# The last group of the down projection: two token tiles one behind the other, and the final weighing on VectorE alone

## The reference

```python
xs = xs + g2x[:, None, :] * _swiglu(_modulate(_rmsnorm(xs, norm2_g[l]), sh2x, sc2x), w_ff1[l], w_ff3[l], w_ff2[l])
...
return _rmsnorm(xs, final_g)          # final norm of every token

def _rmsnorm(x, g):
    xf = x.astype(jnp.float32)
    y = xf * lax.rsqrt(jnp.mean(xf * xf, axis=-1, keepdims=True) + EPS)
    return (y * g.astype(jnp.float32)).astype(x.dtype)
```

## Time and profile before

| | us |
|---|---|
| median of 3 runs | 1735.04 |
| the three runs | 1739.56, 1731.56, 1735.04 |
| the profiled execution | 1731.98 |
| its span | 1730.0 |

### The profile page before, as it was taken

The page is one execution under the profiler, slowest core; times in us unless marked ns, Lnnn a source line. Parts: engine busy times, 40 slices in busy tenths (PEclk is TensorE's granted clock), DMA queues, the critical chain, the costliest instruction groups (busy, mean ns, idle before and its releaser), DMA issues.

```text
span 1730.0 us, 23409 instructions
## 1 busy us (share of the span) xinstructions
PE 1696.5 (98%) x8360; PEld 1428.7 (83%) x8360; DVE 1278.2 (74%) x1809; ACT 689.3 (40%) x1132; POOL 454.4 (26%) x407
## 2 busy tenths in 40 slices
PE   6999999999999999999999999999999999999997
PEld 3798988989898888888888888888888888888885
DVE  6587636565457667776789846888887889789998
ACT  7534241422333213445555414443334333434444
POOL 1002020200212000111121200065463655565551
PEclk9999999999999999999999999999999999999999
DMA  9111110212059133787776634156556555887652
GB/s 343 49 50 37 62 49 25 80 41 74 13 188 310 63 97 111 261 278 251 252 268 207 220 111 146 38 176 229 213 201 248 181 207 206 297 285 247 205 170 98
DMA packets 145424, 284.93 MB, mean 165 GB/s; under 512 B 9362, under 2 KB 96034, under 8 KB 141506
## 3 DMA queue, kind: packets, MB, share of 16 engines
q1 hardware_dynamic: 115314, 177.30, 30.6%
q0 software_dynamic: 30032, 106.59, 17.4%
HBM read 205.68 MB, written 78.17 MB: 164 GB/s over the span
## 4 chain that ended last, share of the span: by engine, by line
PE 87%; DVE 6%; DMA 3%; issue 2%; ACT 1%; SPq 0%; POOL 0%; DVEq 0%; ACTq 0%
PE PD L2493 14%; PE PD L2941 11%; PE PM L2941 11%; PE PM L2816 6%; PE PD L2816 6%; PE PD L2978 5%; PE PM L2978 5%; PE PD L2847 4%; PE PD L2624 4%; PE PD L2509 4%; PE PM L2697 2%; DMA g_ring<-g_dram 2%; PE PD L2637 1%; PE PM L2877 1%; PE PD L2877 1%
## 5 line engine op out<-in xcount | busy, mean ns | idle before, releaser
L1091 POOL TENSOR_TENSOR wm_lo<-wm_lo,wm_hi 128x1024 fp32r<-128x1024 f32 x35 | 92.9, 2666 | 79.5 <-ACT wm_hi L1598 78.9
L2493 PE MATMUL PD<-R_hi,whi 128*128 128x512 f32 x352 | 110.2, 394 | 0.0
L2493 PE MATMUL PD<-R_lo,whi 128*128 128x512 f32 x352 | 108.6, 390 | 0.0
L2493 PE MATMUL PD<-R_hi,wlo 128*128 128x512 f32 x352 | 108.5, 389 | 0.0
L2262 DVE TENSOR_TENSOR ws_lo<-S,ws_hi 128x512 fp32r<-128x512 f32 x76 | 82.7, 1099 | 24.3 <-ACT ws_hi L1533 24.3
L942 POOL TENSOR_TENSOR kw<-ktok,hc 128x1280 f32<-128x1280 f32 x8 | 18.4, 2323 | 286.8 <-DVE ktok L1946 286.8
L1533 ACT ACTIVATE ws_hi<-S 128x512 fp32r<-128x512 f32 x76 | 47.7, 627 | 90.7 <-DVE S L2276 66.3
L2402 DVE TENSOR_TENSOR fm_lo<-fm_lo,fm_hi 128x512 fp32r<-128x512 f32 x70 | 79.1, 1130 | 0.7 <-ACT fm_hi L1605 0.7
L2493 PEld LDWEIGHTS PD<-R_hi,wlo 128*128 128x128 f32 x352 | 66.1, 188 | 14.0
L2493 PEld LDWEIGHTS PD<-R_lo,whi 128*128 128x128 f32 x352 | 66.1, 188 | 13.9
L2493 PEld LDWEIGHTS PD<-R_hi,whi 128*128 128x128 f32 x352 | 65.2, 188 | 12.9 <-issue 0.2
(11 more groups left out here) (532 smaller groups left out, 5353.2 us busy)
## 6 DMA issues: line engine op xcount, KB each, us to landing
rawF<-in_w_ff SPq DMA_DIRECT2D x44, 512.0 KB, 6.2
wm_lo<-w_dram SPq DMA_DIRECT2D x35, 512.0 KB, 3.9
ada<-in_w_ada POOLq DMA_DIRECT2D x32, 512.0 KB, 5.5
raw<-in_w_in SPq DMA_DIRECT2D x30, 512.0 KB, 5.2
g_dram<-snapG POOLq DMA_DIRECT2D x48, 256.0 KB, 4.8
f_dram<-Fo SPq DMA_DIRECT2D x11, 1024.0 KB, 5.6
w_dram<-job_a POOLq DMA_DIRECT2D x20, 512.0 KB, 3.7
fm_lo<-fs_dram SPq DMA_DIRECT2D x40, 256.0 KB, 4.1
```

The costliest lines, as they stand in the source:

```text
L1091: nc.gpsimd.tensor_tensor(lo[:, :, :], lo[:, :, :].bitcast(F32), hi[:, :, :].bitcast(F32), ALU.subtract).then_inc(wm_ready, 1)
L2493: i = mm(dst[:, e * HALF:e * HALF + width], wk[:, k, :], part, start=(k == 0 and step == 0), stop=(k == KT - 1 and step == 2))
```

## The change

- The last group's order becomes all seven products of par 0, then all seven of par 1, each in the order 0, 1, 3, 2, 6, 4, 5. The counts that TensorE and VectorE wait for are adapted to it (`need`, `SAME_IN_LAST`).
- GpSimd's three multiplications and ScalarE's three (L1114, L1673) are gone; VectorE's `write_out` does all eight tiles.
- The factors of tiles 0 and 4 are made in one set of steps on columns 128x2, and so are those of tiles 1 and 5. One set is a RECIPROCAL, two TENSOR_TENSOR and a SCALAR_TENSOR_TENSOR. The other four tiles keep their own set of three.
- The factors move: before they stood behind additions n = 1, 2, 3 and 5; now behind n = 4 and n = 6. The writes of tiles 0, 4, 1, 5 stand behind n = 4, 5, 6, 7.
- Tiles are finished in the order 0, 4, 1, 5, 2, 6, 7, 3. SyncE waits for VectorE alone.

The diff, cut to its core:

```diff
+SAME_IN_LAST = {3: 1, 4: 5, 5: 4}
-LAST_ORDER = ((0, 0), (1, 0), (0, 1), (0, 2), (1, 1), (0, 3), (1, 2), (0, 4), (1, 3), (0, 5), (1, 4), (0, 6),
-              (1, 5), (1, 6))
+LAST_ORDER = tuple((par, p) for par in range(2) for p in (0, 1, 3, 2, 6, 4, 5))
-NORM_TILES = (0, 4, 1, 5, 2, 6, 3, 7)
-POOL_NORMS = 3
+NORM_TILES = (0, 4, 1, 5, 2, 6, 7, 3)
...
-            pool.wait_ge(fg_in, JOBS_IN)
-            for i, t in enumerate(NORM_TILES[0:POOL_NORMS]):
-                pool.wait_ge(normed, i + 2)
-                nc.gpsimd.tensor_tensor(xs2[:, t, :], xs2[:, t, :], fg[:, :], ALU.mult).then_inc(o_pool, 1)
...
-            for i, t in enumerate(NORM_TILES[0:POOL_NORMS]):
-                act.wait_ge(factor, i + 2)
-                nc.scalar.activation(xs2[:, t, :], xs2[:, t, :], ACT.Copy, scale=rs[:, 2, t:t + 1]).then_inc(normed, 1)
-            half_square(2, 0, 0)
-            half_square(6, 1, 1)
-            half_square(3, 0, 2)
-            half_square(2, 1, 0)
-            half_square(7, 1, 3)
-            half_square(6, 0, 1)
-            half_square(3, 1, 2)
-            half_square(7, 0, 3)
+            half_square(0, 0, 3)
+            half_square(1, 1, 6)
+            half_square(1, 0, 7)
+            half_square(0, 1, 8)
+            half_square(3, 0, 3)
+            half_square(2, 1, 6)
+            half_square(2, 0, 7)
+            half_square(3, 1, 8)
...
+                if end == col + 1:
+                    own.link(v.scalar_tensor_tensor(out=root, in0=y, scalar=half, in1=y, op0=ALU.mult, op1=ALU.mult))
+                else:
+                    own.link(v.tensor_tensor(root, y, y, ALU.mult))
+                    own.link(v.tensor_tensor(root, root, half, ALU.mult))
+                own.link(v.scalar_tensor_tensor(out=y, in0=root, scalar=1.5, in1=y, op0=ALU.add, op1=ALU.mult))
...
                 take(END, par, p)
-                if n in (1, 2, 3):
-                    norm_factor(NORM_TILES[n - 1], n).then_inc(factor, 1)
-                if n == 5:
-                    own.link(norm_factor(5, 4))
-                    write_out(5, whole, 5)
+                if n in (4, 6):
+                    norm_factor(n - 4, n - 2, n - 2)
+                if 4 <= n < 8:
+                    write_out(NORM_TILES[n - 4], whole, n - 4)
                 if n == 11:
-                    own.link(norm_factor(LT, 5))
+                    norm_factor(LT + 1, LT + 2, 5)
+                    norm_factor(LT, LT + 1, 6)
                     write_out(2, whole, LT)
-            own.link(norm_factor(LT + 1, 6))
             write_out(6, whole, LT + 1)
-            own.link(norm_factor(LT + 2, 7))
-            write_out(3, whole, LT + 2)
-            own.link(norm_factor(LT + 3, 8))
-            for e in (1, 0):
-                write_out(LT - 1, parts[e], LT + 3)
+            norm_factor(LT + 2, LT + 3, 7)
+            write_out(7, whole, LT + 2)
+            norm_factor(LT + 3, LT + 4, 8)
+            for e in range(2):
+                write_out(3, parts[e], LT + 3)
...
-                before = {0: -2, 1: -1, 2: 1, 3: -4, 4: 3, 5: 2, 6: 0}[p] + G * PRODUCTS_ADDS
+                need = {0: -2, 1: -1, 2: 1, 3: -4, 4: 3, 5: 2, 6: 0}
+                if G == 2 * DU - 1:
+                    need = {0: -2, 1: -1, 3: -4, 2: 1, 6: 0, 4: 4, 5: 2}
+                before = need[p] + G * PRODUCTS_ADDS
```

More of the change, by code:

```diff
@@ L594, in build @@
         taken = [sem(f"taken{k}") for k in range(2)]
-        factor, normed, o_pool = T_mm, wspT_done, mod_ready
         down_hi_d = sem("down_hi_d")
@@ L865, in _ @@
             for i, t in enumerate(NORM_TILES[0:7]):
[L866 to L869, removed]
+                sp.wait_ge(o_ready, i + 2)
                 sp.dma_start(out_t[:, t, :], xs2[:, t, :]).then_inc(out_done, 16)
-            for i, e in enumerate((1, 0)):
+            for e in range(2):
                 at = slice(e * HALF, (e + 1) * HALF)
-                sp.wait_ge(o_ready, LT - POOL_NORMS + 1 + i)
-                sp.dma_start(out_t[:, LT - 1, at], xs2[:, LT - 1, at]).then_inc(out_done, 16)
+                sp.wait_ge(o_ready, LT + 1 + e)
+                sp.dma_start(out_t[:, NORM_TILES[-1], at], xs2[:, NORM_TILES[-1], at]).then_inc(out_done, 16)
             sp.wait_ge(out_done, 16 * (LT + 1))
@@ L1648, in root, with half_square @@
                     .then_inc(root_d, 1)
[L1650 to L1656, removed]
+            def half_square(i, e, adds):
+                t = NORM_TILES[4 + i]
+                first = e == (0 if t < KH else 1)
+                col = (KH if first else LT) + i
+                act.wait_ge(taken[t % 2], (2 * DU - 1) * PRODUCTS_ADDS + adds)
                 own.link(nc.scalar.activation(junkF[:, 0:HALF], xs2[:, t, e * HALF:(e + 1) * HALF], ACT.Square,
@@ L1659, in half_square @@
                 if first:
-                    nc.scalar.activation(last_at[i], rs[:, 0, t:t + 1], ACT.Identity, scale=1.0 / D, bias=eps_at)
-                    own.link(nc.scalar.activation(last_half_at[i], rs[:, 0, t:t + 1], ACT.Identity, scale=-0.5 / D,
-                                                  bias=eps_half_at))
+                    nc.scalar.activation(last_at[i], rs[:, 0, col:col + 1], ACT.Identity, scale=1.0 / D, bias=eps_at)
+                    own.link(nc.scalar.activation(last_half_at[i], rs[:, 0, col:col + 1], ACT.Identity,
+                                                  scale=-0.5 / D, bias=eps_half_at))
                 else:
                     root(col, last_at[i], last_half_at[i])
[L1666 to L1670, removed]
-            for i, t in enumerate(NORM_TILES[0:POOL_NORMS]):
-                act.wait_ge(factor, i + 2)
-                nc.scalar.activation(xs2[:, t, :], xs2[:, t, :], ACT.Copy, scale=rs[:, 2, t:t + 1]).then_inc(normed, 1)
-            half_square(2, 0, 0)
-            half_square(6, 1, 1)
-            half_square(3, 0, 2)
-            half_square(2, 1, 0)
-            half_square(7, 1, 3)
-            half_square(6, 0, 1)
-            half_square(3, 1, 2)
-            half_square(7, 0, 3)
+            for i, t in enumerate(NORM_TILES[0:4]):
+                act.wait_ge(taken[t % 2], (2 * DU - 1) * PRODUCTS_ADDS)
+                own.link(nc.scalar.activation(junkF[:, :], xs2[:, t, :], ACT.Square, accum_out=rs[:, 0, i:i + 1]))
+                root(i, eps_at, eps_half_at)
+            half_square(0, 0, 3)
[6 more added lines that the diff above has]
+            half_square(3, 1, 8)
         @block.vector
@@ L2408, in take @@
                 dve.wait_ge(made[par], of_made[par] + G * PRODUCTS + p + 1)
-                if p in SAME_BEFORE:
-                    dve.wait_ge(taken[par], G * PRODUCTS_ADDS + SAME_BEFORE[p])
+                same = SAME_IN_LAST if G == 2 * DU - 1 else SAME_BEFORE
+                if p in same:
+                    dve.wait_ge(taken[par], G * PRODUCTS_ADDS + same[p])
                 elif p == 0 and G > 1:
@@ L2433, in _, with norm_factor @@
             dve.wait_ge(fg_in, JOBS_IN)
-            def norm_factor(col, roots):
-                root, y, half = (rs[:, k, col:col + 1] for k in (1, 2, 3))
+            def norm_factor(col, end, roots):
+                root, y, half = (rs[:, k, col:end] for k in (1, 2, 3))
                 dve.wait_ge(root_d, 2 * roots + 1)
                 own.link(v.reciprocal(y, root))
-                own.link(v.scalar_tensor_tensor(out=root, in0=y, scalar=half, in1=y, op0=ALU.mult, op1=ALU.mult))
-                return v.scalar_tensor_tensor(out=y, in0=root, scalar=1.5, in1=y, op0=ALU.add, op1=ALU.mult)
+                if end == col + 1:
[4 more added lines that the diff above has]
+                own.link(v.scalar_tensor_tensor(out=y, in0=root, scalar=1.5, in1=y, op0=ALU.add, op1=ALU.mult))
             def write_out(t, at, col):
```

## The result

| | before | changed |
|---|---|---|
| median of 20 runs, us | 1733.95 | 1738.79 |
| lowest and highest | 1729.71, 1742.78 | 1735.10, 1746.03 |
| span of the profiled execution | 1730.0 | 1737.7 |

The ratio is 1.0027, with a 95% interval of 1.0016 to 1.0039. So the change costs 4.8 us where a gain of 2.4 was forecast, and the time lies 1.2 us above the range given. It is small, but with twenty runs on either side the interval lies wholly above 1, so it is no noise.

The account below looks back on a forecast made before the run. TensorE bounds the kernel, VectorE's list the tail: 1703.51 + 21.19 + 0.15 + 0.25 = 1725.10 against 1727.48, 2.4 us earlier. So 1735.04 - 2.4 = 1732.6 us, range 1728.2 to 1737.6.

Parts of the forecast that it names:

- What bounds the tail: Last group from addition n = 4: VectorE's list of work, 21.19 us after the change, sets the end.
- GpSimd's lock, 5.61 us: Behind addition n = 5: GpSimd's SBUF reads hold three two-input VectorE instructions, costing 5.61 us, which the change removes.
- The rival of the output transfers: Same three long VectorE steps: output transfers held them, so 5.61 us comes back, 1738.2 us; chance 4%.
- the priced list: VectorE's instructions from addition n = 4 at 1703.51 us, priced by differences of starts: 23.97 us before, 21.19 after.
- Does TensorE keep up?: Prediction's section on last-group products: TensorE waits 1.8 us before n = 10, VectorE 0.15 us for n = 11.
- TensorE's wait before n = 10: Last group: product n = 10 waits for the addition n = 7, 1.8 us in place of 3.49.
- the two rivals: TensorE's clock in the tail: falls once, up to 1734.2 us, 16%; or low for four last products, 1735.7 us, 3%.
- The sign that I named: Mark of a wrong forecast: VectorE idle for over 1 us behind addition n = 7.
- The chances: Whole kernel against before: faster 6%, slower 4%, the same 90%; about 0.5%, 8.7 us, taken as the limit.
- all cases but one: Forecast and its four priced rivals: all but one said to lie inside 0.5%, even the worst, 3.2 us slower.

Follow-up runs that it names:

- e1_place: Changed kernel, but each last-group addition waits for as many products of its parity as its own place in the list; tail 29.57 us, ratio 0.9994.
- e3_no_pool: Kernel before, with one-column memsets in place of GpSimd's three multiplications by final_g; tail 26.73 us, ratio 0.9974.
- e7_pool_reads: e1_place plus three GpSimd multiplications of a spare buffer beside VectorE's list; tail 36.08 us, one run 1735.82 us.
- e8_pool_writes: e1_place plus three GpSimd memsets of a spare buffer, which write but read nothing; tail 29.58 us, one run 1731.80 us.
- e6_two_by_pool: e1_place's order and waits, but GpSimd and ScalarE weigh tiles 0 and 4 with only VectorE additions beside GpSimd; tail 27.67 us, ratio 0.9968 to before.
- e5_order_alone: e1_place with the final weighing of before, three tiles by ScalarE and GpSimd; tail 33.54 us, ratio 1.0010 to before.
- e2b_only_three: Changed kernel with only the addition of p = 3 waiting for its own place; tail 37.28 us, one run 1738.00 us.

## Why the prediction was wrong

- **What bounds the tail**, VectorE's list: right. The prices hold to a tenth: a double set of factor steps takes 0.77 us (1709.06 to 1709.83) against 0.79, a whole-tile write 1.19 to 1.21, an addition 0.60. In e1_place the list takes 27.11 us from the first addition to its end, where the forecast had 26.95.
- **GpSimd's lock, 5.61 us**: right, shown by taking GpSimd's work away (e3_no_pool, 26.73 where 26.9 was worked out) and by adding it elsewhere (e7_pool_reads). The rival of the output transfers is out: in e8_pool_writes and e1_place they run beside steps of normal length.
- **The step that failed** is that I let each addition start when its own product was ready. It stands in the start of the priced list, n = 4 at 1703.51 as before, and in "Does TensorE keep up?", where the products' results are in VectorE's list as soon as they are made and VectorE waits 0.15 us in all. The change moved the products and left VectorE's wait on p + 1. I worked TensorE's waits out by the new order and did not do the same for VectorE's wait, which the diff leaves alone. From the first addition to VectorE's end the forecast was 29.35 - 2.4 = 26.95 us; measured, 35.23. Of the 8.3 between, 3.1 lie ahead of n = 4 (8.51 us behind the first addition, 5.38 worked out), and 5.2 in the waits inside the list (1.38 + 3.89 + 0.31 = 5.58 by differences of starts, 0.40 worked out). The first two of these waits are for products at the low clock in part; no run separates its share from that of the counts.
- **TensorE's wait before n = 10**: 1.8 forecast; 4.35 measured in the changed kernel and 1.63 with right counts. The rest over 1.63 comes from the late start of VectorE's list, since the addition n = 7 stands 7.56 us behind n = 4 (7.58 worked out).
- **The clock**: the two rivals gave it 0.15 to 1.6 us and 0.6 us over before. It did fall, during a wait of 4.35 us that I had not foreseen. In e1_place, with the wait that I had, it did not.
- **The sign that I named**, idle time of VectorE of over 1 us behind n = 7, did come (1.29 and 3.80 us), but I had it as the mark of some unnamed failure. None of my rivals was a wait that the change leaves in place.
- **The chances**: 90% went to less than 0.5% either way, which the ratio 1.0027 is in. I wrote that all cases but one lie inside 0.5%; by my own numbers all five do. And 0.5% is not the limit of what can be told: with twenty runs on either side the interval is 0.0023 wide. The range was too narrow above by 1.2 us, since it was built from the mechanism that I took for certain and the spread of three runs.

## What to carry to other kernels

When an order is changed, go through every wait on a counter between the two engines, above all those that the diff does not touch: a count that was written as an index is right only in the order of the index. One that asks for too much gives right values and a slow tail. One that asks for too little gives right values only as long as something ahead of it has waited for enough, as here for p = 2, 4 and 5. Then read the timeline for additions that start when some other product ends. And keep GpSimd's reads of SBUF away from VectorE's instructions with two SBUF inputs: in e6_two_by_pool only additions from PSUM stood beside them, no step was held, and both engines were used.

## What was not expected of the hardware

The hold goes both ways. In e7_pool_reads one of GpSimd's three multiplications takes longer than the others, the third:

```profile
L1111 POOL TENSOR_TENSOR job_x<-job_x,fg x3: 2392/2395/3215, 1704.1 to 1709.0; 128x1024 f32<-128x1024 f32 x3
```

The columns are least, median and greatest duration in ns, then the first and last start. The third starts at 1709.0, when the second has ended and VectorE's write of 1706.71, which had waited for the second, gets its turn until 1710.02. The third takes 3.2 us in place of 2.4, and VectorE's next write in turn ends 1.1 us behind it. The durations are those of two engines that take turns, each for a whole instruction. The Trainium skill ("SBUF — State Buffer", section "Who interferes with whom") says that the order of issue decides which of the two engines is blocked, so that GpSimd can be held as well, and that a VectorE instruction with two SBUF inputs contends only with a GpSimd instruction that reads SBUF. This trace agrees with the first and e8_pool_writes with the second.

TensorE's granted clock fell around waits of 3.49, 4.10, 4.35, 4.35 and 6.67 us (before, e5_order_alone, changed, e2b_only_three, e7_pool_reads) and stayed at 1.00 around one of 1.63 us (e1_place). Before, it fell 1.3 us after TensorE had resumed, in the other four while TensorE still waited. It was then low for 3.4 us (before, e5_order_alone) or 6.8 us (the other three), and a product at 0.50 took 2.57 us in place of 1.36.
